# Broadcasts of running sums moved from TensorE to DMA, and side chains spaced further apart

## The reference

```python
# SSD layer, 64 heads in 8 groups, 2 chunks of 128 tokens
da_cs = cumsum(dt * a)                       # running sums, one row per head
decay = exp(where(causal, da_cs[l] - da_cs[s], -inf))
cb = einsum('bclgn,bcsgn->bcgls', cm, bm)
y_diag = einsum('bcgls,bcgels,bcsgep->bclgep', cb, decay, xdt)
# mLSTM: sc = (q k) * exp(dmat - m);  h = rmsnorm(num / max(|den|, exp(-m))) * o
# gla:   chunk states of 32 tokens, o = rmsnorm(q_dec state + scores v) * silu(r)
# diff:  w = softmax(q1 k1) - lam * softmax(q2 k2); o = rmsnorm(w v)
# S5:    64 groups of complex recurrences of 64 states, then gelu and a GLU
```

## Time and profile before

| | |
|---|---|
| median of 3 runs | 3530.93 us (3530.44 to 3531.49) |
| the profiled execution | 3531.95 us, span 3530.1 us |
| PE busy | 3290.6 us, 93% of the span |
| DVE busy | 2315.8 us, 66% |
| ACT busy | 1798.8 us, 51% |
| POOL busy | 672.7 us, 19%, most of it from 1685 to 2460 us |
| mean granted TensorE clock | 0.968 of full speed |
| DMA read from HBM | 542.25 MB |

### The profile page before, as it was taken

How to read it: one execution, slowest core, us unless ns; L and a number is a source line. 1 busy time by engine, 2 the same in 40 slices (tenths; PEclk the granted TensorE clock), 3 DMA queues, 4 the chain that set the end, 5 groups by cost and what they waited for, 6 DMA issues and landing times.

```text
span 3530.1 us, 54486 instructions
## 1 busy us (share of the span) xinstructions
PE 3290.6 (93%) x21902; PEld 2961.2 (84%) x21902; DVE 2315.8 (66%) x3229; ACT 1798.8 (51%) x2313; POOL 672.7 (19%) x1118
## 2 busy tenths in 40 slices
PE   6999878999999999999889888989999999999998
PEld 5889777889888888888878777878999888888887
DVE  6655766656666666576666666666556788888544
ACT  4444666544555555544455444333444566666443
POOL 1000000010000000011567765885000100000000
PEclk9999988999999999999999998999999999999999
DMA  4445333655434344455433333344655655555554
GB/s 169 155 136 169 112 114 122 204 190 187 136 131 131 132 132 137 164 182 196 163 109 114 114 114 107 127 132 147 206 185 173 197 191 190 190 189 190 186 191 142
DMA packets 148749, 552.08 MB, mean 156 GB/s; under 512 B 16512, under 2 KB 16512, under 8 KB 147856
## 3 DMA queue, kind: packets, MB, share of 16 engines
q1 hardware_dynamic: 148496, 548.61, 46.9%
HBM read 542.25 MB, written 6.29 MB: 155 GB/s over the span
## 4 chain that ended last, share of the span: by engine, by line
PE 72%; DVE 10%; POOL 8%; ACT 6%; issue 2%; DMA 1%; SPq 0%; DVEq 0%; ACTq 0%; POOLq 0%
PE ps L543 72%; POOL TB L1909 4%; DVE WL L1313 2%; POOL PT L1909 2%; ACT L880 2%; ACT WH L890 1%; POOL BX L1909 1%; POOL SQ L1909 1%; POOL BS L1909 1%; ACT SQ L880 1%; DMA RAW<-in_w 0%; DVE XC L1287 0%; DVE X L1287 0%; DVE BS L1303 0%; DMA scratch<-X 0%
## 5 line engine op out<-in xcount | busy, mean ns | idle before, releaser
L543 PE MATMUL ps<-XN,WH 128*128 128x256 f32 (+1 forms) x8864 | 1900.7, 308 | 78.3 <-DVE WL L1313 31.1
L890 ACT ACTIVATE WH<-RAW 128x1024 fp32r<-128x1024 f32 x1010 | 1064.3, 1057 | 1391.5 <-PE ps L543 1349.8
L1313 DVE TENSOR_TENSOR WL<-RAW,WH 128x1024 fp32r<-128x1024 f32 x1010 | 1253.1, 1244 | 566.6 <-ACT WH L890 559.9
L543 PEld LDWEIGHTS ps<-XN,WH 128*128 128x128 f32 x8864 | 1463.6, 196 | 184.0 <-issue 47.9
L543 PE MATMUL ps<-XN,WL 128*128 128x256 f32 x5120 | 1459.7, 285 | 0.0
L543 PEld LDWEIGHTS ps<-XN,WL 128*128 128x128 f32 x5120 | 997.5, 195 | 0.0
L543 PE MATMUL ps<-YS,WH 128*128 128x512 f32 (+1 forms) x1088 | 374.9, 390 | 10.3 <-DVE ZB L1276 6.0
L1909 POOL TENSOR_TENSOR RSB<-RSB,SQ 128x256 f32<-128x256 f32 x75 | 86.6, 1154 | 1341.8 <-ACT SQ L880 1340.8
L543 PE MATMUL ps<-YS,WL 128*128 128x256 f32 x1056 | 295.6, 280 | 0.0
L543 PEld LDWEIGHTS ps<-YS,WH 128*128 128x128 f32 x1088 | 202.8, 189 | 58.9 <-DVE ZB L1276 7.1
L1909 POOL TENSOR_TENSOR SQ<-SQ 128x256 f32<-128x256 f32 (+1 forms) x32 | 33.6, 1051 | 1144.8 <-ACT SQ L880 1143.3
(11 more groups left out here) (332 smaller groups left out, 3482.9 us busy)
## 6 DMA issues: line engine op xcount, KB each, us to landing
RAW<-in_w SPq DMA_DIRECT2D x1010, 512.0 KB, 3.4
scratch<-X SPq DMA_DIRECT2D x2, 2048.0 KB, 7.4
X<-scratch SPq DMA_DIRECT2D x2, 2048.0 KB, 8.6
X<-in_x SPq DMA_DIRECT2D x4, 512.0 KB, 9.0
X<-in_x SPq DMA_DIRECT2D x1, 2048.0 KB, 10.4
out<-X SPq DMA_DIRECT2D x4, 512.0 KB, 2.6
WIF<-in_w_if SPq DMA_DIRECT2D x1, 576.0 KB, 7.0
CV<-in_vec SPq DMA_DIRECT2D x1, 543.5 KB, 3.9
```

Of the source, the lines that this page charges most:

```text
L543: return pe.e.matmul(dst, l, r, start=start, stop=stop, skip_group_check=True)
L890: act.e.activation(WH[:, w % NW, :], RAW[:, w % NRAW, :], ACT.Copy).then_inc(*act.one(("wh", w)))
L1313: dve.e.tensor_tensor(WL[:, w % NW, :], RAW[:, w % NRAW, :], WH[:, w % NW, :].bitcast(F32), SUB).then_inc(*dve.one(("wl", w)))
```

## The change

Two things are changed.

First, in the SSD layer, the running sums no longer reach all partitions through PE. SP stores `CSX` once to HBM (`sums`), and for each of the 64 heads a DMA reads the row of 256 sums into 128 partitions, in a ring of five buffers `CSB`. ACT then takes `Relu(cs[s] - cs[l])` in two pieces and one `Exp` with scale -1 over both; the mask, before added by PE, is now in `CBm`, which DVE makes once per group as `cb` times a triangle `TRI`, where ACT copied it before. SP waits for `csr` of head h before it loads head h + 5. All later steps of `ssd` come one step earlier (16 steps in place of 17). `CSX` and `DTR` now share `ZB`'s memory, so the first `zs` evacuation waits for the store.

Second, the chains are spaced further: `heads` 12 to 16 steps a head, `gla` 14 to 18, `diff` 10 to 15, an `s5` pair 10 to 11 units (197 steps). The plan's `End("diff")` come later, and `g12`, `gb`, `db` tiles go in pairs.

```diff
-    "tail": 6, "heads": 48, "eo": 1, "dt": 1, "dts": 6, "xv": 1, "zs": 1, "ssd": 17, "oo": 1, "nx": 4,
-    "s5c": 7, "u": 1, "al": 1, "gv": 1, "gq": 1, "gk": 1, "gr": 1, "dec": 7, "gla": 14, "lam": 3,
-    "dv": 1, "dq": 1, "diff": 10, "g12": 1, "gb": 1, "db": 1, "g0": 1, "gg": 1, "gl": 2, "s5": 181, "wo": 1,
+    "tail": 6, "heads": 64, "eo": 1, "dt": 1, "dts": 6, "xv": 1, "zs": 1, "ssd": 16, "oo": 1, "nx": 4,
+    "s5c": 7, "u": 1, "al": 1, "gv": 1, "gq": 1, "gk": 1, "gr": 1, "dec": 7, "gla": 18, "lam": 3,
+    "dv": 1, "dq": 1, "diff": 15, "g12": 1, "gb": 1, "db": 1, "g0": 1, "gg": 1, "gl": 2, "s5": 197, "wo": 1,
...
-        else:
-            p.append(End("diff", (h - 1,)))
+        elif h > 1:
+            p.append(End("diff", (h - 2,)))
         p.append(Go("diff", (h,)))
-    for n in range(16):
-        for c in range(2):
-            p.append(whole(tile("g12", (n, c), "w_in_2", 7184 + 2048 * (c + 1) + 128 * n), 16))
-        if n == 0:
+    p.append(End("diff", (2,)))
+    for m in range(0, 16, 2):
+        for n in (m, m + 1):
+            for c in range(2):
+                p.append(whole(tile("g12", (n, c), "w_in_2", 7184 + 2048 * (c + 1) + 128 * n), 16))
+        for n in (m, m + 1):
+            p.append(whole(tile("gb", (n,), "gla_w_br_2", 128 * n, "gos"), 8))
+        if m == 0:
             p.append(End("diff", (3,)))
-        p.append(whole(tile("gb", (n,), "gla_w_br_2", 128 * n, "gos"), 8))
-        p.append(whole(tile("db", (n,), "diff_w_br_2", 128 * n, "dos"), 8))
+        for n in (m, m + 1):
+            p.append(whole(tile("db", (n,), "diff_w_br_2", 128 * n, "dos"), 8))
...
-                h, s = divmod(s, 12)
+                h, s = divmod(s, 16)
...
-                if 1 <= s <= 8:
-                    e_ = s - 1
-                    h = 8 * g + e_
-                    b = take("side", "bc", g, e_)
-                    pe.wait_ge(*at("dts"))
-                    mm(b[:, 0:384], identr, maskr, True, False)
-                    mm(b[:, 0:384], ident[0:64, h:h + 1].to_broadcast([64, 128]), CSX, False, True).then_inc(
-                        *pe.one(("bc", g, e_)))
-                if 4 <= s <= 11:
-                    e_ = s - 4
+                if 3 <= s <= 10:
+                    e_ = s - 3
...
-                    act.wait_ge(*at("bc", g, e_))
+                    b = CSB[h % NCSB]
+                    act.wait_ge(csb_in[h % NCSB], 16 * (h // NCSB + 1))
...
-                    fn(d[:, 0:256], b[:, 0:256], ACT.Exp, bias=NCST[:, h:h + 1])
-                    fn(d[:, 256:384], b[:, 256:384], ACT.Exp, ("dec_", g, e_), ("free", "bc", g, e_),
-                       bias=NCST[:, 64 + h:65 + h])
+                    fn(d[:, 0:256], b, ACT.Relu, bias=CST[:, h:h + 1], scale=-1.0)
+                    fn(d[:, 256:384], b[:, 128:256], ACT.Relu, ("csr", g, e_), bias=CST[:, 64 + h:65 + h], scale=-1.0)
+                    fn(d, d, ACT.Exp, ("dec_", g, e_), scale=-1.0)
...
+                    dve.wait_ge(*at("cb", g))
+                    tt(CBm, bank("cb", g)[:, 0:384], TRI, MUL, ("free", "cb", g))
...
-                if s == 12:
+                if s == 11:
...
+            def csb(h):
+                if h < 64:
+                    sp.e.dma_start(CSB[h % NCSB], sums[h:h + 1, :].to_broadcast([128, 256])).then_inc(csb_in[h % NCSB], 16)
+            def dts(s):
+                if s == 4:
+                    sp.wait_ge(*at("csx"))
+                    load(sums, CSX, "cst")
+                if s == 5:
+                    sp.wait_ge(*at("cst"))
+                    sp.wait_ge(*at("st1"))
+                    for h in range(NCSB):
+                        csb(h)
+            def ssd(g, s):
+                if 1 <= s <= 8:
+                    e_ = s - 1
+                    sp.wait_ge(*at("csr", g, e_))
+                    csb(8 * g + e_ + NCSB)
...
-        r = s - (10 + 10 * (n // 2) + 5 * (n % 2))
+        r = s - (11 + 11 * (n // 2) + 5 * (n % 2))
```

More of the change, by code:

```diff
@@ L18 @@
 NEG = -1.0e30
+NCSB = 5
 TWO_PI = 6.283185307179586
@@ L330, in flat, with build @@
     return ap.rearrange("p a b -> p (a b)")
-def build(nc, args, out, scratch):
+def build(nc, args, out, scratch, sums):
     ctx = ExitStack()
@@ L404, in build @@
         YS2 = v3(m("YS2", 32 * 512, F32R), 32)
-        CSX = m("CSX", 384, rows=64)
-        DTR = m("DTR", 256, rows=64)
-        NCST = m("NCST", 128)
+        CST = m("CST", 128)
         DTT = m("DTT", 128)
         ZB = v3(m("ZB2", 4 * 256), 4)
+        CSX, DTR = ZB[0:64, 0, :], ZB[0:64, 1, :]
         XDT = v3(m("XDT", 1024), 2)
@@ L415, in build @@
         XV1 = v3(m("XV1", 6 * 256), 6)
+        CSB = [m(f"CSB{i}", 256) for i in range(NCSB)]
         assert m.at <= XT + 2048
@@ L493, in build @@
         raw_in = [sem(f"raw_in{i}") for i in range(NRAW)]
-        loads = ["cv", "cs", "wif", "x1", "st1", "x2", "st2", "b1", "b2", "c1", "c2", "wg", "db", "x3"]
+        csb_in = [sem(f"csb_in{i}") for i in range(NCSB)]
+        loads = ["cst", "cv", "cs", "wif", "x1", "st1", "x2", "st2", "b1", "b2", "c1", "c2", "wg", "db", "x3"]
         loads += [f"x0{q}" for q in range(4)]
@@ L796, in gla @@
                     i.then_inc(*pe.one(("gs", h)))
-                if 3 <= s <= 6:
-                    p = s - 3
+                if 5 <= s <= 8:
+                    p = s - 5
                     b = take("side", "kv", h, p)
@@ L816, in gla @@
                     i.then_inc(*pe.one(("go", h)))
-                if s == 12:
+                if s == 16:
                     kept.discard(holder_of("go", h))
-                if s == 10:
+                if s == 14:
                     b = take("side", "gn", h)
@@ L867, in tensor @@
             walk(block, lambda u: None, {
-                "consts": consts, "nend": nend, "q": q, "k": k_, "v": v, "gates": gates, "heads": heads, "dts": dts,
+                "nend": nend, "q": q, "k": k_, "v": v, "gates": gates, "heads": heads, "dts": dts,
                 "ssd": ssd, "rst": rst, "ring3": ring3, "ring4": ring4, "s5": s5, "dec": dec, "gla": gla, "lam": lam,
@@ L1068, in ssd @@
             def ssd(g, s):
-                if s == 0:
-                    act.wait_ge(*at("cb", g))
-                    if g:
-                        act.wait_ge(*at("msk", g - 1, 7))
-                    fn(CBm, bank("cb", g)[:, 0:384], ACT.Copy, ("cbm", g), ("free", "cb", g))
-                if 2 <= s <= 9:
-                    e_ = s - 2
-                    h, d, b = 8 * g + e_, DB[e_ % 3], bank("bc", g, e_)
-                    act.wait_ge(*at("bc", g, e_))
+                if 1 <= s <= 8:
+                    e_ = s - 1
+                    h, d = 8 * g + e_, DB[e_ % 3]
+                    b = CSB[h % NCSB]
+                    act.wait_ge(csb_in[h % NCSB], 16 * (h // NCSB + 1))
                     if 8 * g + e_ > 2:
@@ L1365, in consts @@
             def consts():
-                copy(identr, ident)
-                copy(maskr, cs("mask"), ("maskr",))
+                ts(TRI, cs("mask"), 0.0, None, ALU.is_ge, None)
             def xm(h, j, s):
@@ L1544, in dts @@
                     ts(RT[3], DTR, EA, -1.0, MUL, MUL)
-                    scan(CSX[:, 0:256], ONE64, RT[3], 0.0, MUL, ADD)
-                    copy(CSX[:, 256:384], CSX[:, 128:256], ("csx",))
+                    scan(CSX, ONE64, RT[3], 0.0, MUL, ADD, ("csx",))
                 if s == 5:
@@ L1549, in dts @@
                     b = bank("dtt")
-                    ts(NCST, b[:, 0:128], -1.0, None, MUL, None)
+                    copy(CST, b[:, 0:128])
                     copy(DTT, b[:, 128:256], ("dts",), ("free", "dtt"))
@@ L1559, in zs @@
             def zs(g, j, s):
+                if g == 0 and j == 0:
+                    dve.wait_ge(*at("cst"))
                 evac(ZB[:, j, :], 1, "zs", g, j, more=[("zsr", g)])
@@ L1714, in gla @@
                        ("free", "gs", h))
-                if 4 <= s <= 7:
-                    p = s - 4
+                if 6 <= s <= 9:
+                    p = s - 6
                     dve.wait_ge(*at("kv", h, p))
@@ L1931, in heads @@
             def heads(s):
-                h, s = divmod(s, 12)
-                if s == 5:
+                h, s = divmod(s, 16)
+                if s == 8:
                     pool.wait_ge(*at("hsqr", h))
@@ L2073, in sync @@
             walk(lambda t, k, a, b: None, unit, {
-                "x1": x1, "st1": st1, "x2": x2, "s5l": s5l, "st2": st2, "wg": wg, "dbl": dbl, "x3": x3, "last": last})
+                "x1": x1, "st1": st1, "dts": dts, "ssd": ssd, "x2": x2, "s5l": s5l, "st2": st2, "wg": wg, "dbl": dbl, "x3": x3, "last": last})
         for engine in (tensor, scalar, vector, gpsimd, sync):
@@ L2195, in program @@
     scratch = nc.dram_tensor("scratch_0", (128, 16, 256), F32).ap()
-    build(nc, args, out, scratch)
+    sums = nc.dram_tensor("sums_0", (64, 256), F32).ap()
+    build(nc, args, out, scratch, sums)
 def kernel(**inputs):
```

98 lines of the change are left out of this document (48 added, 50 removed).

## The result

| | before | after |
|---|---|---|
| median, us | 3530.73 (3530.44 to 3531.49) | 3486.06 (3483.85 to 3487.05) |
| profiled span, us; mean clock of TensorE | 3530.1; 0.96 | 3485.3; 0.96 |

The ratio is 0.9872, 95% interval 0.9855 to 0.9889: faster by 44.7 us. I had forecast 145 us, and the range, 3315 to 3462, did not hold the time.

The account below looks back on a forecast made before the run. PE, busy 93% of the span, was taken as the bound, with POOL setting the pace in the later s5 pairs. 3531.95 - 36 (SSD) - 40 (heads) - 69 (s5, gla, diff) = 3387, so median 3386 us; range 3315 to 3462.

Parts of the forecast that it names:

- SSD: SSD stage: 64.6 us from removed broadcasts, less 12 for longer waits and 16 for half clock, gains 36 us.
- 64.6: SSD: PE time of the removed broadcast products, 1.01 us a head over 64 heads, counted in full.
- the step by itself: SSD chain one step earlier: seven SQ waits of 3.9 us in place of 2.16 cost 12 us, half clock 16.
- Rivals 2, 4 and 5: In SSD: 2, VectorE's late WL, 3422 us, chance 0.12; 4, Relu reloads, 3450, 0.03; 5, slow broadcast DMA, 3559, 0.03.
- a wait of 4 us costs more than itself, one of 2 us doesn't: PE's clock: a wait near 4 us brings half clock after it; SSD's waits of about 2.2 us left it at 1.00.
- `heads`: Heads stage: spacing removes 27 of 54 us of waits and 34 us at half clock, gaining 40 us, bounds 15 and 65.
- The argument for `EB` and `SQ`: Heads: EB gains one position (2.9 us), SQ two (5.8 us); their waits fall from 18 to about 3 us.
- First part of s5, `gla`, `diff`: 1745 to 2156 us: PE bounds it; of 72 us lost to waits and half clock, 18 stay and 54 are gained.
- Second part: 2156 to 2527 us: wider s5 pairs at 39.9 us, 352 us against 371, 19 gained.
- `diff` 3's end: Before db: the third diff chain's end costs as much as ZS, 4 us, but where POOL bounds.
- `ZS`: End of s5 on the last step: DVE's ZS piece and a WL stand before gg, 4 us lost.
- The first rival: s5 stretch: POOL keeps its pace everywhere, spaced chains win nothing beside it; 3455 us, chance 0.15.

Follow-up runs that it names:

- e1: The kernel before with only the sums by DMA and the 16-step SSD chain, no chain spaced further; 3496.2 us, ratio 0.9901 to before.
- e3: The kernel after with the end of each SSD chain one step later, so 17 steps again; 3459.8 us, ratio 0.9798 to before.
- e10: The kernel after with the heads chain's period at 17 steps in place of 16; 3485.7 us, ratio 0.9875 to before.
- e12: The kernel after with the second zl tile of each gate group behind the four short ra and ix tiles; 3499.8 us, ratio 0.9909 to before.
- e16: The kernel after with two VectorE products of the heads stage (HB by OZ, scan result by ZB) on GpSimd; 3494.7 us, ratio 0.9896 to before.
- e13: The kernel after with the third diff chain's forced end behind the first branch tiles, not ahead; 3474.5 us, ratio 0.9840 to before.
- e9: The kernel after with each tile's last s5 step (HH products and VectorE's use of them) one step later; 3459.8 us, ratio 0.9801 to before.
- e11: The kernel after with four edits: SSD chain end later, gla and diff halves' adds and one BX product on VectorE, HH later; 3396.1 us, ratio 0.9621 to before.
- e5: The kernel after with s5 pairs every 10 units again, gla and diff still spaced, sums by DMA; 3464.8 us, ratio 0.9809 to before.
- e8: The kernel after with one of GpSimd's two BX products behind the scan moved to VectorE; 3467.1 us, ratio 0.9818 to before.

## Why the prediction was wrong, step by step

**SSD: right, in part by luck.** Forecast 36 us, measured 35.6 (e1) and 37 (stages). A head's unit is 3.86 us. The waits for `SQ` grew by 15 us, forecast 12. The half clock grew from 3 to 44 us, x 0.45 = 18, forecast 16, and a new wait for `DB` took 2.5. From 64.6 that leaves 29, and the stage gave 37: 8 us came that no term of mine names, and they hid that the costs were too low. e3 says the step by itself costs 26, forecast 28. No wait for `CSB`, no reload for `Relu`, ScalarE hidden. Rivals 2, 4 and 5 did not happen.

One premise beside it fell: "a wait of 4 us costs more than itself, one of 2 us doesn't". In e3 seven of the eight waits for `SQ`, of 1.9 us each, go with 3.4 us at the lower clock level (1.2 GHz), where seven of 2.2 us before went with none.

**`heads`: the failed step is "I take 27 of the 54 us of waits and 34 of the 61 to 64 us at half clock away".** The stage gave about 6 us of 40: the waits went from 54 to 51 us, and the mean clock stayed at 0.90. The argument for `EB` and `SQ` was right: 18.2 us of them became 2.1. I booked a wait removed as time gained. `WL` and `ZB` went from 15.7 to 32.6 us; I read this as PE reaching the gate groups earlier and finding them as unready as before. e10, e12 and e16 show that three different edits don't lower the sum.

**First part of s5, `gla`, `diff`: "I leave 18 (a POOL at nearly 90% is often late) and gain 54" failed in size.** Up to unit 563 it gained 25 us. Of its losses 45 us of waits and 55 us at half clock are left, where before had 56 and 68. The waits named, `DS` and others, did shrink; `SQ` stayed (14.6 us before, 16.3 now), and `HH`, `RS` and `WL` make 23. Missing was the count of steps at the forced ends: 15 steps, with 8 units under them for `diff` 2 and 10 for `diff` 3. What spacing adds to a chain is taken back there with no units between. I named `diff` 3's end, at 4 us, and left it out of the sum; it waited 14.0, and `diff` 2's 9.0. e13 puts a price on one of these ends: 12 us.

**Second part: "352 against 371, 19 gained" failed, with the wrong sign.** It lost 19. By weight units the 62 with phases took 259 us before and the 36 behind them 110; after has 78 and 20, at 321 and 67. The term that failed is 283 us for 7.1 pairs, "7.1 x 39.9", which measured 321. Of the 38 us too few, the forced wait of `diff` 3 is 14, and a pair took 43.9 to 44.7 us, not the 39.9 that GpSimd's load seemed to set. I looked only at the engine's load and not at the order in which PE issues: at 11 the odd tile's last step and the next pair's first coincide, and the late one stands first. e9 gives the pair its order back and gets 41.0 us, e11 39.9. So GpSimd's pace was read rightly, and is what an unblocked chain runs at. The units that no longer lie behind the chain were also priced too high, 124 - 69 = 55 us for 16 of them, where before took 2.9 us for such a unit. Against pairs of 10, e5 puts the loss at 21 us, `ZS` included.

**`ZS`: right**, 3.0 us of wait against 4 us lost.

The first rival, that spaced chains win nothing beside GpSimd, came nearest (3455), with half the right cause: beside it `heads` won little either, and the s5 spacing lost. Among the rivals was none in which a wider chain lies beside more units and loses there what it had gained, which is what happened to the s5 chain.

## What to carry to other kernels

A wait removed from an engine's queue is time gained only if the next thing in that queue is ready. Before booking it, add up all the waits of the stage and ask which cause is left when PE arrives earlier; if every name is a different short answer of the same busy engines, book little. When a software pipeline's period changes, write out which steps of successive items now share a slot and in which order they are issued, and count the steps that a forced end must run with nothing beside them. A wider period also makes the chain longer: count the units that it newly lies beside, and price them at what a unit costs with the chain less what one costs without. To see where time went, cut both traces at the same unit of work.

## What the runs showed of the hardware that was not expected

VectorE and GpSimd in work at the same time can turn a relief into nothing. In e16 GpSimd took 1.73 and 2.88 us for products that VectorE does in 0.73 and 1.23, and VectorE's own operation on `YS` went from a mean of 547 ns to 759. It is the overlap: in e16 the 18 of these 24 that ran with GpSimd idle took 0.50 us on the mean and at most 0.70, the 6 beside a GpSimd operation 1.54 and at least 1.06; for `WL` it is 1.22 (63 of them) against 1.46 (13). Groups of VectorE, 344 to 662 us, first of after and then of e16:

```profile
L1266 DVE TENSOR_TENSOR YS<-XC,YS 128x256 fp32r<-128x256 f32 (+1 forms) x24 | 13.1, 547 | 2.7 <-ACT YS L874 0.4
```

```profile
L1266 DVE TENSOR_TENSOR YS<-XC,YS 128x256 fp32r<-128x256 f32 (+1 forms) x24 | 18.2, 759 | 2.8 <-ACT YS L874 0.4
```

In e8, too, GpSimd lost two products of some 1.2 us a pair, and its busy time in four pairs behind the forced end fell only from 34.8 to 34.1 us on the mean: its other operations grew. The Trainium skill (SBUF — State Buffer, on the shared port pair) has a VectorE operation with two inputs and a GpSimd operation that reads SBUF exclude each other for a whole instruction; the direction of both runs agrees (0.50 against 1.54 us), and the prediction had used that rule only for one more `WL` a pair.

The clock after equal waits differed. In after a wait of 3.6 to 4.7 us for `HH` was followed by 10.2 us at the lower level (1.2 GHz), five times of six; in e5 waits of 3.4 to 5.0 us by 3.4 or 6.8. In before seven waits of 2.2 us for `SQ` went without it, in e3 seven of 1.9 us came with 3.4 us each. No run here tells why.
